# Differential attention on VectorE: ratio and combination of the former pair behind the first maximum instead of behind the second

## The reference, cut to what matters

```python
s1 = jnp.einsum('bqhd,bkhd->bhqk', a, k1).astype(jnp.float32) * scale
s2 = jnp.einsum('bqhd,bkhd->bhqk', b, k2).astype(jnp.float32) * scale
p = jax.nn.softmax(s1, axis=-1) - lam * jax.nn.softmax(s2, axis=-1)
return jnp.einsum('bhqk,bkhd->bqhd', p.astype(v.dtype), v)
```

## Time and profile before

| | us |
|---|---|
| median of 3 runs | 3074.38 |
| the runs | 3074.01 to 3077.2 |
| the profiled execution | 3066.51 |
| its span in the trace | 3064.8 |
| the differential attention in it, first to last maximum | 2518.4 to 2710.1 |

### The profile page before, as it was taken

One profiled execution on the slowest core, in us unless ns is written; L12 is line 12 of the kernel. 1 busy time (PEld: TensorE's weight loads), 2 busy tenths in 40 slices (PEclk: granted clock), 3 DMA queues, 4 the chain that ended last, 5 costly groups with the idle time before them and its releaser, 6 DMA issues.

```text
span 3064.8 us, 47759 instructions
## 1 busy us (share of the span) xinstructions
PE 2911.5 (95%) x17540; PEld 2508.7 (82%) x17540; DVE 1622.3 (53%) x3106; ACT 1161.2 (38%) x2101; POOL 1069.8 (35%) x690
## 2 busy tenths in 40 slices
PE   7999998999999999999999999999999987789999
PEld 6689866778888888888999988997897986678887
DVE  3899838343222232313029278982212959988861
ACT  3311264242212211213124356772322635557750
POOL 2223020432222235662225433444331544332335
PEclk9999998999999999999999999999999999999999
DMA  4123331431111113442297444313335863131223
GB/s 144 60 98 126 109 78 29 138 117 49 48 48 48 48 55 91 137 164 82 93 211 227 118 109 101 83 58 125 135 138 180 239 163 72 49 76 35 72 88 129
DMA packets 219514, 319.44 MB, mean 104 GB/s; under 512 B 81286, under 2 KB 163078, under 8 KB 217174
## 3 DMA queue, kind: packets, MB, share of 16 engines
q1 hardware_dynamic: 184774, 273.10, 30.0%
q10 hardware_dynamic: 33360, 39.98, 3.8%
q0 software_dynamic: 1216, 4.20, 0.5%
HBM read 225.76 MB, written 91.47 MB: 104 GB/s over the span
## 4 chain that ended last, share of the span: by engine, by line
PE 70%; DVE 9%; issue 3%; ACT 1%; POOL 1%; SPq 0%; DMA 0%; DVEq 0%; POOLq 0%; ACTq 0%; PEldq 0%
PE psum L2575 16%; PE psum L530 15%; PE psum L2356 8%; PE psum L2778 8%; PE psum L1085 4%; PE psum L1116 4%; PE psum L1096 3%; PE psum L794 3%; DVE arena L3195 3%; PE psum L772 2%; PE psum L783 2%; DVE diff L1475 1%; PE psum L1390 1%; PE psum L1367 1%; DVE arena L3184 1%
## 5 line engine op out<-in xcount | busy, mean ns | idle before, releaser
L2575 PE MATMUL psum<-parts_ffn 128*128 128x512 f32 x2112 | 482.0, 391 | 3.8 <-DVE parts_ffn L2532 3.8
L2575 PEld LDWEIGHTS psum<-parts_ffn 128*128 128x128 f32 x2112 | 398.2, 189 | 87.2 <-issue 2.2
L530 PE MATMUL psum<-parts_even,parts_ffn 128*128 128x256 f32 x2496 | 305.0, 285 | 3.0 <-DVE parts_ffn L2919 1.8
L530 PEld LDWEIGHTS psum<-parts_even,parts_ffn 128*128 128x128 f32 x2496 | 302.8, 193 | 3.4 <-DVE parts_ffn L2919 2.0
L2645 DVE SCALAR_TENSOR_TENSOR arena<-psum,arena 128x1023 f32<-128x1023 f32 x88 | 112.9, 1283 | 328.2 <-ACT arena L2629 322.0
L530 PE MATMUL psum<-parts_odd 128*128 128x248 f32 x2304 | 270.5, 280 | 2.7 <-DVE parts_odd L2532 1.8
L530 PEld LDWEIGHTS psum<-parts_odd 128*128 128x128 f32 x2304 | 268.3, 190 | 3.8 <-DVE parts_odd L2532 2.0
L576 ACT ACTIVATE arena<-psum 128x256 f32<-128x256 f32 (+2 forms) x240 | 87.5, 375 | 392.5 <-PE psum L530 388.7
L444 PE MATMUL psum<-parts_mixer 128*128 128x512 f32 x912 | 210.2, 391 | 0.3 <-DVE parts_mixer L287 0.3
L444 PEld LDWEIGHTS psum<-parts_mixer 128*128 128x128 f32 x912 | 170.7, 188 | 35.8 <-DVE parts_mixer L287 0.5
L2102 DVE TENSOR_SCALAR_CACHE_REDUCE choose_flags<-arena,choose_bits 128x384 uint8<-128x384 f32 (+2 forms) x198 | 174.3, 942 | 1.2
(11 more groups left out here) (370 smaller groups left out, 5889.5 us busy)
## 6 DMA issues: line engine op xcount, KB each, us to landing
arena<-ffn_up_b SPq DMA_DIRECT2D x44, 512.0 KB, 3.2
arena<-ffn_down_k SPq DMA_DIRECT2D x44, 512.0 KB, 3.7
arena<-x SPq DMA_DIRECT2D x8, 2048.0 KB, 8.7
arena<-w_in_e SPq DMA_DIRECT2D x13, 1024.0 KB, 6.7
e_tokens<-arena ACTq DMA_DIRECT2D x26, 512.0 KB, 3.1
x<-arena SPq DMA_DIRECT2D x24, 512.0 KB, 3.7
arena<-w_in_o SPq DMA_DIRECT2D x12, 992.0 KB, 6.6
o_tokens<-arena ACTq DMA_DIRECT2D x24, 496.0 KB, 3.0
```

The lines of the kernel that those rows point to most:

```text
L530: last = pe.matmul(self.bank(t), self.hT[:, a, k, t * P:(t + 1) * P], self.weights.parts[:, self.weights.slot(s), b, k, :], start=(k, a, b ...
L2575: last = pe.matmul(self.core.psum[:, 4 * u + 2 * s + h, :], parts[:, s, a, k, :], self.hT[:, b, k, h * HALF:(h + 1) * HALF], start=(k, a, ...
```

## The change

In every iteration VectorE does weigh(m-1) and combine(m-1) right behind peak(m, 0) and its addition, ahead of low(m-2) and of peak(m, 1). Before, they stood behind peak(m, 1). No instruction is added or taken away, and no wait is changed; the other engines' orders stay. The condition on `BY_POOL` goes too; that tuple is empty, so it never held.

```diff
             if m < M:
                 self.peak(dve, m, 0)
+            if 0 <= m - 1 < M:
+                self.weigh(dve, m - 1)
+                self.combine(dve, m - 1)
             for h in range(2):
                 if 0 <= m - 2 < M:
                     self.low(dve, m - 2, h)
             if m < M:
                 self.peak(dve, m, 1)
-            if 0 <= m - 1 < M:
-                self.weigh(dve, m - 1)
-                if (m - 1) % TT not in self.BY_POOL:
-                    self.combine(dve, m - 1)
             if m % 2 and 0 <= m - 7 < M:
                 self.finish(dve, (m - 7) // 2)
```

## The result

The changed kernel took 3085.59 us, the median of 7 runs (3084.72 to 3089.7), against 3074.38 for the kernel before (7 runs, 3072.85 to 3078.78). The ratio is 1.0041, with a 95% interval from 1.0032 to 1.0051: slower by 0.4%, where I had forecast no change that can be told.

The account below looks back on a forecast made before the run. The loop was taken as bound by a chain through VectorE, ScalarE and TensorE, 11.45 us a pair. Terms 5.2 - 3.5 - 0.5 - 2.2 = -1.0 us gave 3073.4 from 3074.4, range 3067 to 3080.

Parts of the forecast that it names:

- head: Loop's first iterations: remainders' wait for ScalarE goes (1.4 us), first combination meets a subtraction (up to 1.3 more); sum -0.5 us.
- pairs, at full clock: Steady loop, iterations 6 to 30: the longer chain makes a pair 11.85 us against 11.45, +5.2 us over 13 pairs.
- collisions in the steady loop: VectorE's combinations lengthened by GpSimd's SBUF subtractions: 3.4 left of 6.9 us, so -3.5 us, bounds -6.9 and +1.2.
- tail, from the last first maximum to L1085: Loop's end: last maximum to last transposes 3.2 us less, 1 us more for GpSimd: -2.2 us, bounds -3.2 and -1.
- the new chain: Even iterations: second maximum through ScalarE and TensorE to the next first maximum 7.57 us, then VectorE 4.28: 11.85 a pair.
- my rivals: Chain not lengthened (3064.3, chance 0.08), no more collisions (3067.5, 0.09), weigh waits (3083, 0.08), worst collisions (3081, 0.05), nothing moves (inside forecast).
- The rival in which weigh waits: VectorE stands still before weigh for the second exponential's sum, 0.3 us a tile, 9.6 over 32 tiles: 3083 us, chance 0.08.
- the near tie in the earlier trace: At 2615.99 the combination began 0.03 us before GpSimd's subtraction yet lasted 3.45 us; so close a start doesn't count as first.

Follow-up runs that it names:

- three arrangements of the filling: Changed kernel with 8 useless TensorE transposes in even iterations ahead of second scores and attend (1.0002), only attend (stretch 206.1 us), or only second scores (206.2 us).
- both changed orders: ScalarE's take at the start of even iterations, in the changed kernel (0.997) and with VectorE's second maximum ahead of the remainders (0.9965), ratios to before.

## Why the prediction was wrong

The terms of the sum, against the first pair of profiles. The steady loop is taken from the first maximum of iteration 7 to that of iteration 31, 12 pairs: 144.6 us before, 154.9 after.

| term | forecast | measured |
|---|---|---|
| head (to iteration 7) | -0.5 | -0.4 |
| pairs, at full clock | +5.2 (13 of +0.40) | +4.3 (12 of +0.36) |
| collisions in the steady loop | -3.5 | -5.9 (6.9 to 1.0) |
| TensorE's low clock | not in the sum | +12.2 |
| tail, from the last first maximum to L1085 | -2.2 | +0.3 |
| sum | -1.0 | +10.5 (the stretch: +10.2) |

**The step that failed** is the new chain, where it took "to attend 0.47, to scores 1.50, to the maximum 1.13" from rows at full clock. I had read a granted clock of 1.00 for the middle of the loop and carried it over to an order that leaves TensorE idle otherwise. The chain through the engines was right: 11.81 us in each pair with a clock of 1.00, in three arrangements of the filling too, where I had worked out 11.85, and a wait of 0.65 us (start to start) where I had 0.70. But in 7 of 12 pairs attend and the scores behind it ran at the lower level, and these two lie on the chain: 13.35 against 11.81, and 13.83 in the pairs where attend took 2.90 and the scores 1.91 us. Summed over the 7 pairs, without their long combinations, it is 12.2 us, more than the whole loss. None of my rivals held it, and so the range ended at 3080. The rival in which weigh waits gave a time near the result (3083), but its mechanism did not come: before L1483 VectorE waited once, 0.9 us, for the last tile.

What could have been seen: in the changed order TensorE's idle times follow from the chain, 1.6 us in front of the second scores and 1.2 in front of attend, with one set of scores between. And the one pair with a low clock in the steady loop before is that in which long combinations lengthened TensorE's idle time (3.42 us in front of the transposes at 2619.50), with two of the four in the earlier trace rows:

```profile
2611.78:2627.24 15.46, 10.57 (x60) 8.54 (x58) 14.70 (x17) 7.15 (x13) 15.01 (x9) 0.89 0.51 172
```

The page "TensorE: Matmul & The Clock Gate" of the Trainium skill (section "What's actually happening") has the two levels, 1.2 GHz as that of an idle engine. Here it fell in a loop whose pairs at full clock have the engine at work for 9.0 of 11.8 us.

**The tail** was a term counted wrong, in two ways. I summed the loop from first maximum to first maximum, and the tail from the last second maximum; but combine(30) had not gone, it had moved ahead of that maximum: first to second maximum of iteration 31 is 4.30 us after, 2.58 before. And I followed only VectorE to the last transposes. In TensorE's queue attend stands ahead of them:

```profile
2733.28 2.83 PE L1390 MATMUL psum<-both,diff 128*128 128x256 f32 x12 [3.01 <-issue]
2735.91 0.63 PE L1401 MATMUL psum<-arena,diff 128*128 128x128 f32 x2
2736.33 1.25 PE L1377 MATMUL psum<-arena,both 128*128 128x128 f32 x8
```

It waited for take, behind the last exponential and the rounded parts, and then ran at the lower level. From the last maximum (2729.48) the transposes begin after 6.85 us, where I had 4.9 plus 1 for GpSimd. Some 5.5 of it would be left at full clock.

**The collisions** came out better than I took them: of the changed kernel's combinations in the steady loop two were long, by 0.3 and 0.7 us, 1.0 in all where I had left 3.4. The sign was right and the size inside its bounds (-6.9 to +1.2); the failed step in it is what I made of the near tie in the earlier trace rows. The changed loop has two more of them. VectorE and then GpSimd in order of time, after (start, duration, engine):

```profile
2577.89 1.28 DVE L1493 SCALAR_TENSOR_TENSOR both<-diff,diff,both 128x1024 f32<-128x1024 f32 x1
...
2630.47 1.28 DVE L1493 SCALAR_TENSOR_TENSOR both<-diff,diff,both 128x1024 f32<-128x1024 f32 x1
```

```profile
2577.96 3.45 POOL L1315 TENSOR_TENSOR diff_even<-diff,diff_even 128x1024 fp32r<-128x1024 f32 x1
...
2630.56 3.45 POOL L1315 TENSOR_TENSOR diff<-diff,diff 128x1024 fp32r<-128x1024 f32 x1
```

Here the combination began 0.07 and 0.09 us ahead of the subtraction and kept its 1.28 us, and it was the subtraction that took 3.45 us in place of 2.36. Each would have cost VectorE about 2.2 us had it gone as at 2615.99 before; that is more than the 2.4 us by which the term was off. The rule that I had weighed against that row (the Trainium skill, "SBUF — State Buffer", section "SBUF: two separate sides": whoever starts first gets the port pair for the whole instruction) is what these rows show; the near ties go against it. Over all thirteen profiles, and with the trace's starts taken to three places, the combination lost at 0.004, 0.031 and 0.046 us ahead (the last in the second profile of before, 3.46 us), and won in all 24 cases from 0.055 to 0.241. All three that it lost were against the subtraction of L1308, which it otherwise beat from 0.146 us on, while the wins from 0.055 to 0.106 are against other lines, L1315 nearly always. So the runs don't tell whether the edge lies at 0.05 us for all, or is another one for L1308.

**The head** was right in its sum, -0.4 us, but not in its parts. The remainders' waits that went were 1.2 us, near my 1.4. The long combinations there cost 2.4 us where they had cost 0.2, and I had allowed 1.3 at most. By these two alone the head would be 1.0 us longer; the 1.4 us that make up the difference are not accounted for, so that term's agreement is luck.

## What to carry to other kernels

An engine that is not the busiest can still lose its own speed, as TensorE did here: when an order is changed, work out where TensorE will stand idle, how long and with how much work between, and price the matmuls behind that on the chain at the lower clock as a rival. Where two engines hand a chain to each other, as here, try not to have the instruction that the other waits for last in an iteration, but behind it something that is waited for later (here the remainders). And take a copy that only frees a bank out of the queue behind slow work: take went ahead of the rounded parts and the first exponential and brought both changed orders to VectorE's own 11.15 us a pair, and the order before to 11.24.

## What the runs showed of the hardware

TensorE's granted clock fell to the lower level though in the changed kernel's steady loop the engine was never idle for more than 1.7 us at a time: two idle stretches of 1.6 and 1.2 us around 1.2 us of work did it in 7 and 8 of 12 pairs, of 1.3 and 1.2 around 1.2 in 6 of 12, of 1.7 and 0.9 us around 1.5 in 5 of 12, and of 1.7 and 0.3 us, or 0.7 and 1.2, in none. Why it took some pairs and spared others with the same instructions at the same distances is left open. Matmuls without use were enough to hold the clock: 16 a pair, at 0.13 us each, were worth 12 us by the runs, and with 8 a pair one profile each shows a stretch some 12 us shorter too.

Where a combination on VectorE began 0.055 us or more ahead of GpSimd's subtraction, it always kept its own duration, and the subtraction took 0.9 to 1.1 us more; at 0.046 us and less it was the combination that took 2.1 to 2.2 us more. A combination that began while a subtraction ran ended 1.08 or 1.09 us behind the subtraction's end in 76 of 82 cases, wherever in it it had begun; the other six began in its last 0.06 us and kept their 1.28.
